# Scan instructions for the gates' running sums, running maxima and chunk recurrence in a two-layer hybrid decoder trunk

## What is computed

```
log_i = i_pre + b_i;  log_f = log_sigmoid(f_pre + b_f)
bcum = cumsum(lf, axis=3)                          # inside each chunk of 128
log_d = where(causal, bcum[.., :, None] - bcum[.., None, :] + li[.., None, :], -inf)
m_row = maximum(log_inter, max(log_d, axis=-1))    # a running maximum of li - bcum, plus bcum
m_new = maximum(bl_n + m_st, a_n)                  # over the chunks, one after the other
```

## Time and profile before

| | |
|---|---|
| median of three runs | 2682.59 us (2678.79 to 2685.31) |
| the profiled execution: its own time | 2680.53 us |
| its span in the trace | 2678.7 us |
| PE busy | 95% of the span |
| DVE busy | 55% |
| POOL busy | 48% |
| ACT busy | 27% |
| mean granted TensorE clock | 0.979 |

### The profile page before, as it was taken

One profiled execution on the slowest core, in us unless ns is written; L12 is line 12 of the kernel. 1 busy time (PEld: TensorE's weight loads), 2 busy tenths in 40 slices (PEclk: granted clock), 3 DMA queues, 4 the chain that ended last, 5 costly groups with the idle time before them and its releaser, 6 DMA issues. The chain is left out here.

```text
span 2678.7 us, 29947 instructions
## 1 busy us (share of the span) xinstructions
PE 2553.2 (95%) x12004; PEld 2091.5 (78%) x12004; DVE 1486.5 (55%) x1822; ACT 716.3 (27%) x1098; POOL 1279.8 (48%) x739
## 2 busy tenths in 40 slices
PE   7899998999999989999998999999999999899997
PEld 5688776878888878887776877678888888788875
DVE  6977755664343443354778677476543434424556
ACT  3020214243333330123222020332433333211132
POOL 4332231448788754443433323223688888444431
PEclk9999999999999999999999999999999999999998
DMA  4221102112323251311132110121223232422111
GB/s 153 73 68 51 48 32 79 55 63 71 95 73 93 71 196 49 124 50 45 47 120 75 54 46 32 35 84 48 79 72 94 75 91 75 170 104 69 48 48 63
DMA packets 60602, 202.31 MB, mean 76 GB/s; under 512 B 8104, under 2 KB 16552, under 8 KB 56240
## 3 DMA queue, kind: packets, MB, share of 16 engines
q1 hardware_dynamic: 32544, 116.41, 13.8%
q10 hardware_dynamic: 27920, 83.99, 8.8%
HBM read 161.02 MB, written 32.54 MB: 72 GB/s over the span
## 5 line engine op out<-in xcount | busy, mean ns | idle before, releaser
L1699 POOL TENSOR_TENSOR w_hi<-w_raw,zero 128x1024 fp32r<-128x1024 f32 (+1 forms) x145 | 272.1, 1876 | 1143.5 <-PE proj L1754 1128.8
L1752 PE MATMUL proj<-h_hi,w_hi 128*128 128x512 f32 x1792 | 717.2, 400 | 51.2 <-DVE conv_raw L668 21.7
L1753 PE MATMUL proj<-h_hi,w_lo 128*128 128x512 f32 x1792 | 704.4, 393 | 0.0
L1754 PE MATMUL proj<-h_lo,w_hi 128*128 128x512 f32 x1792 | 704.1, 393 | 0.0
L1752 PEld LDWEIGHTS proj<-h_hi,w_hi 128*128 128x128 f32 x1792 | 341.0, 190 | 131.7 <-issue 53.8
L1753 PEld LDWEIGHTS proj<-h_hi,w_lo 128*128 128x128 f32 x1792 | 341.1, 190 | 71.0 <-issue 2.6
L1754 PEld LDWEIGHTS proj<-h_lo,w_hi 128*128 128x128 f32 x1792 | 340.2, 190 | 72.0
L1703 POOL TENSOR_TENSOR w_lo<-w_raw,w_hi 128x1024 fp32r<-128x1024 f32 (+1 forms) x145 | 387.3, 2671 | 11.4
L986 DVE TENSOR_TENSOR x<-x,proj 128x512 f32<-128x512 f32 x128 | 87.7, 686 | 328.5 <-PE proj L1754 328.5
L1710 POOL TENSOR_TENSOR w_lo<-w_raw,w_hi 128x512 fp32r<-128x512 f32 x120 | 183.6, 1531 | 113.0 <-ACT w_hi L1303 113.0
L1710 POOL TENSOR_TENSOR w_lo<-turns,w_hi 128x512 fp32r<-128x512 f32 x120 | 180.4, 1504 | 62.9 <-ACT w_hi L1303 62.9
(11 more groups left out here) (278 smaller groups left out, 4396.7 us busy)
## 6 DMA issues: line engine op xcount, KB each, us to landing
w_raw<-weights SPq DMA_DIRECT2D x170, 512.0 KB, 3.2
act_spill<-act ACTq DMA_DIRECT2D x44, 512.0 KB, 5.2
turns<-weights SPq DMA_DIRECT2D x40, 512.0 KB, 4.1
h_whole<-act_spill ACTq DMA_DIRECT2D x12, 1024.0 KB, 9.4
ffn_b_whole<-act_spill ACTq DMA_DIRECT2D x8, 1024.0 KB, 6.4
w_raw<-weights SPq DMA_DIRECT2D x16, 384.0 KB, 3.0
x<-x_in ACTq DMA_DIRECT2D x8, 512.0 KB, 8.3
ml_d<-rows_spill ACTq DMA_DIRECT2D x64, 64.0 KB, 3.3
```

Of the source, the lines that this page charges most:

```text
L1699: g.tensor_tensor(whi[:, slot, 0:n], w, zero1[:, 0:1].to_broadcast([P, n]), ALU.add).then_inc(w_hi_made, 1)
L1752: pe.matmul(out, wh, rhi, start=first, stop=False)
L1753: pe.matmul(out, wl, rhi, start=False, stop=False)
L1754: return pe.matmul(out, wh, rlo, start=False, stop=final)
```

## The change

`running` gets a destination, a source, a row of constants and two operations, and issues one `tensor_tensor_scan` for each of the eight chunks, 4x128 elements each. For column j the scan computes state = (constant_j op0 state) op1 source_j and writes the state. The row C_KEEP is 0 in column 0 and 1 elsewhere (multiply, then add: a running sum); C_DROP is -1e30 in column 0 and 0 elsewhere (add, then maximum: a running maximum). DVE waits once, after the last of the eight. The seven steps of line 734 become one scan over seven columns. `VEC_STEPS` falls from 283 to 265. The tile of constants grows by 256 columns a partition. Nothing else moves: each call stands where it stood, and writes the same tile as before.

```
-VEC_STEPS = 283
+VEC_STEPS = 265
-            def running(L, src, bufs, op):
-
-                for i in range(7):
-                    sh, dst = 1 << i, bufs[i % 2]
-                    a = src.rearrange("p (n c) -> p n c", c=CHUNK)
-                    o = dst.rearrange("p (n c) -> p n c", c=CHUNK)
-                    v.tensor_copy(o[:, :, 0:sh], a[:, :, 0:sh]).then_inc(vec_step.sem, 1)
-                    count()
-                    v.tensor_tensor(o[:, :, sh:], a[:, :, sh:], a[:, :, 0:CHUNK - sh], op).then_inc(vec_step.sem, 1)
-                    v.wait_ge(vec_step.sem, step_at(L))
-                    src = dst
-                return src
+            def running(L, dst, src, first, op0, op1):
+
+                for n in range(NCH):
+                    o = slice(CHUNK * n, CHUNK * n + CHUNK)
+                    v.tensor_tensor_scan(dst[:, o], const[0:MH, first:first + P], src[:, o], 0.0, op0, op1).then_inc(vec_step.sem, 1)
+                    at = step_at(L)
+                v.wait_ge(vec_step.sem, at)
...
-                running(L, m_[2][R4], [m_[3][R4], m_[4][R4]], ALU.add)
+                running(L, m_[3][R4], m_[2][R4], C_KEEP, ALU.mult, ALU.add)
...
-                running(L, u, [m_[4][R4], m_[2][R4]], ALU.max)
+                running(L, m_[4][R4], u, C_DROP, ALU.add, ALU.max)
...
-                for n in range(NCH - 1):
-                    v.scalar_tensor_tensor(mprev[:, n + 1:n + 2], mprev[:, n:n + 1], cm3[:, n, CHUNK - 1:],
-                                           bc3[:, n, CHUNK - 1:], ALU.max, ALU.add).then_inc(vec_step.sem, 1)
-                    v.wait_ge(vec_step.sem, step_at(L))
+                v.tensor_tensor_scan(mprev[:, 1:NCH], cm3[:, 0:NCH - 1, CHUNK - 1], bc3[:, 0:NCH - 1, CHUNK - 1], 0.0,
+                                     ALU.max, ALU.add).then_inc(vec_step.sem, 1)
+                v.wait_ge(vec_step.sem, step_at(L))
...
+    c[:, C_KEEP:C_KEEP + P] = np.where(i > 0, 1.0, 0.0)[None, :]
+    c[:, C_DROP:C_DROP + P] = np.where(i > 0, 0.0, -1e30)[None, :]
```

More of the change, by code:

```diff
@@ L62 @@
 C_XI = C_DEC + RH * P
-C_ZETA = C_XI + PAIRS * P
+C_KEEP = C_XI + PAIRS * P
+C_DROP = C_KEEP + P
+C_ZETA = C_DROP + P
 C_GAM = C_ZETA + RH
```

## The result

| | kernel before | changed kernel |
|---|---|---|
| median | 2683.95 us (2678.79 to 2686.7, 4 runs) | 2654.79 us (2653.32 to 2655.23, 4 runs) |
| the profiled execution | 2680.53 us, span 2678.7 | 2655.23 us, span 2653.4 |
| mean granted TensorE clock | 0.979 | 0.981 |

The ratio is 0.9893 with a 95% interval of 0.9875 to 0.991: 29 us, or 1.1%, faster. The forecast was 2655, range 2650 to 2672.

What follows compares the result with a forecast made beforehand. PE's matmuls bound the kernel, but in this stretch DVE does, with `running` ahead of PE's banks. Two layers at 13.3 us less: 2680.53 - 26.6 = 2653.9, given as 2655 for the median; range 2650 to 2672.

Steps and rivals of the forecast that it cites:

- What bounds the stage: Units 4 to 9, each layer: PE waits for evacuations behind `running`; with low clock, 28.1 us at most to win.
- The price of a scan: A 128-column scan on DVE costs two passes, 2.08 ns a column: 0.41 us, 0.34 from start to start.
- DVE's work: Scans in both running parts and the recurrence take 13.1 us of DVE work off each layer.
- POOL's holds stay: Five pairs of POOL's splits still fall before unit 7's evacuation, each holding DVE some 3.3 us, before and after.
- Unit 9: PE still waits 0.7 us a layer for unit 7's first half; unit 9 ends 13.3 us earlier in each layer.
- The end: Whole kernel: 2680.53 less 26.6 gives 2653.9; as the median is compared, 2655 was said.
- Edits at nothing: Constants grow by 128 KB and land 1.9 us later, covered by 20 us before PE's first read: no cost.
- 7 us or less from line 718 to unit 3's evacuation: Sign in the changed profile that the forecast is right: unit 3's evacuation begins within 7 us of line 718.
- Rival A: Stall moves to unit 9, where POOL's sixth pair of splits holds DVE: 2659 to 2671, chance 0.23.
- B: Rival: a scan is no cheaper than what it replaces, only the recurrence gains: 2678 to 2682, chance 0.06.
- C: Rival: slower, each column's carry goes far through the engine; at 2.0 us a scan 2707, chance 0.03.
- The rest of the layer shifts with PE: Everything after unit 9 in each layer (values, rows to columns, mLSTM chunks) moves earlier by the same 13 us.

Runs made afterwards that it cites:

- the second experiment: Scans for the running maximum only, running sum and recurrence as in the kernel before: 2680.34 us, ratio 0.9995 to that kernel.
- the late row: Changed kernel with the recurrence back in its seven steps and the row m_row computed twice: 2667.29 us, ratio 0.9943 to the kernel before.
- the sum alone, the first experiment: Scans for the running sum only, running maximum and recurrence as in the kernel before: 2673.21 us, ratio 0.9964 to that kernel.
- the recurrence alone: Only the seven recurrence steps become one scan, both running parts as in the kernel before: 2682.79 us, ratio 1.0001 to that kernel.

## Why the prediction was right, point by point

- **What bounds the stage.** Right. PE waited for banks behind `running`, and with the waits gone the 28.2 us between units 3 and 9 are the 28.1 the prediction found as the ceiling. That the low clock was part of the price shows in the units (2.7 and 1.7 us behind unit 7's waits) and in PE's busy time, 4.4 us less for the same matmuls.
- **The price of a scan.** Right: 0.39 us for 0.41, 0.32 from start to start for 0.34, 2.11 ns a column for 2.08. Eight take 2.62 us where none is held (the second experiment, 103.71 to 106.33 in its trace) for 2.84.
- **DVE's work.** 13.1 us a layer were written. Unit 7's evacuation moved by 69.63 - 54.94 = 14.7. The recurrence gave 1.5, the running parts about 6.05 each, 13.6 in all; the last 1.1 is a difference in holds, 15.5 us for 16.6 by the long instructions of both timelines.
- **POOL's holds stay.** Right in number up to unit 7's evacuation, five pairs before and after. It was wrong for unit 5's, which I had at 101.9 and which came at 98.56: one of the four pairs that once came before it now comes after. The step that failed is "That of unit 5 begins 11.7 earlier", which carried the old holds along, though the fourth pair of the prediction's own list, at 103.4, lies behind its 101.9. It cost the sum nothing, since PE wanted that bank only at 103.6.
- **Unit 9.** I left 0.7 us of wait a layer; none was there, as DVE was 1.4 us earlier than written. That makes 1.4 of the 1.6 us between the 26.6 forecast and the 28.2 found.
- **The end.** 2655 was met to 0.2 us, and that closeness is luck. The saving of 26.6 taken off the median of that time, 2682.59, gives 2656.0, off the profiled execution 2653.9, and 2655 is a choice between the two. Against it stand 29.2 us between the medians and 25.3 between the profiled executions: the stage gave 1.6 us more than forecast, and the rest of the profiled execution took back 2.9, of which 2.3 are the read-back wait and 0.3 were there before the stage.
- **Edits at nothing.** Right: the larger tile of constants landed 15.0 us after its issue for 14.5, and unit 3 ended 0.24 us later.
- **One sign was written wrong.** "7 us or less from line 718 to unit 3's evacuation" was measured at 7.74. It went against the prediction's own schedule, in which 76.1 less line 718's start at 68.35 makes 7.75, and the schedule was right.
- **Rival A**, the stall that moves to unit 9, didn't happen here, but it is no paper case. The second experiment and the late row show it in both layers, the sum alone in layer 1, and the distance to it was small: DVE work of 2.7 us more a layer (the late row) loses 12 us. Its price was well sized there, 5.6 us of wait where 5 to 7 were written, with the low clock after it. (The 2.8 us written for the low clock in layer 0 are 2.7 by the earlier trace rows: 23.15 - 10.88 - 9.57.) That POOL's splits are what holds DVE is read from ends that coincide and from where the holds move with PE's pace; no run took the splits away. **B and C** fell with the scan's duration.
- **The rest of the layer shifts with PE.** It did here, to 2.9 us: what is left of the span outside the two stretches is 2520.0 us before and 2522.9 changed. Over all ten traces it is 2516.5 to 2526.2, more than the 3 us by which the read-back wait varies. PE's wait for `diag` differs too (3.4 us for the late row, 7.2 before and changed, 11.0 for the recurrence alone); why these waits differ was not looked into. So a span of one trace says little about a difference of a few us, and the small ones above are read from the stretch alone.

## What to carry to other kernels

A share of 55% says nothing of a stage: look for the instruction that stands ahead of the evacuation PE waits for, and time the units themselves, with idleness and low clock in them, to get the ceiling of what can be won. Where two engines hold each other up at moments set by a third one's pace, work taken off is not time taken off: here the scans of one running part alone were worth a third of the whole or nothing. Before trusting such a gain, write down which holds fall ahead of each deadline in the new schedule, and how far the last instruction is from the next one.

## What the hardware showed that was not expected

- A much shorter wait brings the low clock than the 9.57 us of the kernel before. After 3.43 us of idleness the granted clock of the next 5 us is 0.50 in layer 0 of the first experiment and 0.68 in its layer 1, and after 3.14 us it is 0.66. What the low clock costs doesn't go by the length of the wait: 3.1, 1.9 and 1.8 us there, 2.7 and 1.7 behind the 9.57 and 9.59 us of the kernel before. After 0.69 and 1.26 us it stays at 1.00. No experiment put a wait between 1.3 and 3.1 us into this stretch; elsewhere in the changed kernel's trace it is 1.00 also after waits of 1.42, 1.55 and 1.72 us.
- A scan's cost doesn't end with its rate: held by POOL, one of 387 ns took 2551, and a scan of 2278 that had begun first made POOL's split of 1.89 us take 3.57. What counted in these runs was not which instruction was held but whether that was before or after an evacuation that PE waited for.
